# Scores over 64 rows of unpadded keys, a layer norm root per row spread by transposes, two projection units between transposes

## What is computed

```python
hx = rms_norm(x, norm1_g[l]) * (1 + sc1) + sh1
xa_b, xa_c, xa_x, xb_u, xq_g, xk_g, xv_g, xq_w, xk_w, xv_w = split_proj(hx @ w_in[l])
ya, yb = conv_mixers(xa_b, xa_c, xa_x, xb_u, ...)   # yb = silu(layer_norm(dwconv(g) + bias, ln_g, ln_b))
q_g = apply_rope(rms_norm(heads(xq_g), qn_c_g[l]), cos, sin)    # 4 query heads of 64, 2 key heads
o_g = global_attn(q_g, k_g, heads(xv_g), kc_g, vc_g)            # all 512 + 256 keys
o_w = window_attn(q_w, k_w, heads(xv_w), kc_w, vc_w, sink_d[l]) # neighbouring blocks + 256 keys
x = x + g1 * (jnp.concatenate([ya, yb, o_g, o_w], axis=-1) @ w_out[l])
x = x + g2 * hier_moe(rms_norm(x, norm2_g[l]) * (1 + sc2) + sh2, ...)  # 32 experts, 2 per token
```

## Time and profile before

| | us |
|---|---|
| median of 3 runs | 1939.59 (1939.04 to 1943.37) |
| the profiled execution | 1938.68 |
| its span | 1936.8 |
| PE busy | 1672.5 (86%) |
| DVE busy | 689.6 (36%) |
| ACT busy | 322.4 (17%) |
| mean granted TensorE clock | 0.955 of full |

### The profile page before, as it was taken

The page is one execution under the profiler, slowest core; times in us unless marked ns, Lnnn a source line. Parts: engine busy times, 40 slices in busy tenths (PEclk is TensorE's granted clock), DMA queues, the critical chain, the costliest instruction groups (busy, mean ns, idle before and its releaser), DMA issues.

```text
span 1936.8 us, 27043 instructions
## 1 busy us (share of the span) xinstructions
PE 1672.5 (86%) x9982; PEld 985.4 (51%) x9983; DVE 689.6 (36%) x1676; ACT 322.4 (17%) x709; POOL 206.7 (11%) x324
## 2 busy tenths in 40 slices
PE   4999998989969999999795799799969979777773
PEld 2555445754556556665352444476446645444441
DVE  2093655661452212222122477564351111111112
ACT  3110115550210000000000301364110000000000
POOL 0000000000012212222111000000002211111111
PEclk9999998999969999999998799899969999999997
DMA  9347156001259999899998621100169999999994
GB/s 384 143 196 329 66 213 261 1 1 44 92 221 425 426 426 426 341 425 424 428 424 336 246 98 76 44 1 1 76 242 426 425 426 426 425 426 426 426 424 185
DMA packets 51369, 524.57 MB, mean 271 GB/s; under 512 B 10696, under 2 KB 11368, under 8 KB 21872
## 3 DMA queue, kind: packets, MB, share of 16 engines
q1 hardware_dynamic: 33968, 481.51, 59.3%
q0 software_dynamic: 14624, 31.80, 4.3%
q10 hardware_dynamic: 2720, 10.49, 1.4%
HBM read 515.08 MB, written 25.95 MB: 279 GB/s over the span
## 4 chain that ended last, share of the span: by engine, by line
PE 61%; DMA 29%; DVE 7%; ACT 2%; issue 1%; POOL 0%; ACTq 0%; POOLq 0%; DVEq 0%
DMA ring<-in_e_down_dram 25%; PE ps L757 22%; PE ps L534 9%; PE ps L563 7%; PE ps L703 6%; PE ps L598 3%; PE ps L629 2%; PE ps L613 2%; PE ps L484 2%; PE ps L601 2%; DMA xres<-in_ctx_tokens_dram 1%; DMA r<-y_dram 1%; PE ps L745 1%; PE ps L493 1%; PE ps L682 1%
## 5 line engine op out<-in xcount | busy, mean ns | idle before, releaser
L757 PE MATMUL ps<-ring,r 128*64 128x256 f32 (+1 forms) x3920 | 534.2, 427 | 80.4 <-DMA ring<-in_e_up_dram 33.7
L757 PEld LDWEIGHTS ps<-ring,r 128*64 128x64 f32 x3920 | 309.7, 138 | 290.0 <-issue 132.6
L757 PE MATMUL ps<-r 128*64 128x256 f32 (+1 forms) x1760 | 238.2, 423 | 31.7 <-DMA r<-in_e_up_dram 14.1
L1349 DVE TENSOR_TENSOR r<-r,ps 128x128 f32<-128x128 f32 x142 | 34.5, 284 | 540.2 <-PE ps L757 540.2
L757 PEld LDWEIGHTS ps<-r 128*64 128x64 f32 x1760 | 141.1, 137 | 121.0 <-issue 54.5
L534 PE MATMUL ps<-r,ring 128*128 128x512 f32 (+1 forms) x480 | 179.3, 534 | 3.2 <-ACT r L1472 1.6
L563 PE MATMUL ps<-ring,r 128*128 128x512 f32 (+1 forms) x384 | 155.9, 560 | 0.0
L703 PE MATMUL ps<-ring,r 128*128 128x512 f32 x320 | 140.2, 594 | 2.2 <-ACT r L1622 2.2
L534 PEld LDWEIGHTS ps<-r,ring 128*128 128x128 f32 x480 | 92.0, 194 | 93.7 <-issue 87.5
L1369 DVE TENSOR_TENSOR r<-ps,r 128x512 f32<-128x512 f32 x71 | 49.1, 692 | 215.7 <-PE ps L757 215.7
L1645 ACT ACTIVATE r<-ps 128x256 f32<-128x256 f32 x71 | 27.2, 383 | 559.2 <-PE ps L757 559.2
(11 more groups left out here) (192 smaller groups left out, 1480.9 us busy)
## 6 DMA issues: line engine op xcount, KB each, us to landing
ring<-in_e_gate_dram SPq DMA_DIRECT2D x44, 2048.0 KB, 33.1
ring<-in_e_up_dram SPq DMA_DIRECT2D x44, 2048.0 KB, 35.1
ring<-in_e_down_dram SPq DMA_DIRECT2D x44, 2048.0 KB, 35.5
ring<-in_w_mod_dram SPq DMA_DIRECT2D x24, 2048.0 KB, 17.5
r<-in_e_gate_dram SPq DMA_DIRECT2D x20, 2048.0 KB, 35.9
r<-in_e_up_dram SPq DMA_DIRECT2D x20, 2048.0 KB, 38.1
r<-in_e_down_dram SPq DMA_DIRECT2D x20, 2048.0 KB, 38.4
ring<-in_w_in_dram SPq DMA_DIRECT2D x8, 2048.0 KB, 20.4
```

The source lines that it names most:

```text
L757: mm = pe.matmul(ps[g * B:(g + 1) * B, bank, 0:width], x, w[:, k, g * width:(g + 1) * width], start=(k == first), stop=(k == last), tile_p ...
```

## The change

Queries and keys of one head are read from 64 of the 128 partitions of qT and kT with a row tile of the array (`tile_position=(kv * HD, 0)`); `kT_pad`, its clearing and its copies are gone, and the score banks of even and odd units are exchanged. The sums of squares for the layer norm come out as one column per tile with tokens on the rows; root and reciprocal are taken over 128 x 6 elements, and transposes of that column, repeated over 128 columns, spread it behind unit 10 into the banks from which `ln_scale` reads. DVE's two first maxima stand ahead of the rotation of unit 11, and in layer 0 PE's last `mod_turn` stands behind scores 0. In layer 1, units 0 and 1 run on PE between the transposes of tiles 1 and 2 and of tiles 3 and 4, DVE rotates them ahead of `glu_product`, and the ring gets its pieces in the new order. The core of the diff:

```diff
     if layer:
-        return conv + qkv
+        return qkv[:QKV_AHEAD] + conv + qkv[QKV_AHEAD:]
...
+        def score_bank(u):
+            return 2 - u % 2 * 2
...
+                if layer and u < QKV_AHEAD:
+                    pe.wait_ge(h1_act, h1_count(layer, False) + u + 1)
+                    pe.wait_ge(h1_vec, h1_count(layer, True) + u + 1)
...
-                if u >= 1:
+                if u >= (1 + QKV_AHEAD if layer else 1):
                     qk_transposes(layer, u - 1)
...
-                    src = catT[:, 2:4, :]
...
                     pe.wait_ge(ln_sq, 2 * layer + 2)
-                    src = square
+                    for t in range(tiles_of(layer)):
+                        for i in range(2):
+                            mm = pe.matmul(ps[:, 2, t:t + 1], square[:, i, t * P:(t + 1) * P], ones[:, 0:1],
+                                           start=(i == 0), stop=(i == 1))
+                    mm.then_inc(ln_psum, 1)
+                    return
...
                     for i in range(2):
-                        mm = pe.matmul(ps[:, 2 + j, 0:tn], ones, src[:, i, t0:t0 + tn], start=(i == 0), stop=(i == 1))
+                        mm = pe.matmul(ps[:, 2 + j, 0:tn], ones, catT[:, 2 + i, t0:t0 + tn], start=(i == 0), stop=(i == 1))
+                mm.then_inc(ln_psum, 1)
+            def ln_spread(layer):
+                pe.wait_ge(ln_rstds[layer], 1)
+                for t in range(tiles_of(layer)):
+                    mm = pe.transpose(ps_flat[:, 1024 + t * P:1024 + (t + 1) * P],
+                                      ln_rstd[:, t:t + 1].to_broadcast([P, P]), ident)
                 mm.then_inc(ln_psum, 1)
...
-                q = qT[:, group * 2 + r, i * P:(i + 1) * P]
-                bank = (u % 2) * 2
+                rows = slice(kv * HD, (kv + 1) * HD)
+                q = qT[rows, group * 2 + r, i * P:(i + 1) * P]
+                bank = score_bank(u)
...
-                if u == 0 or u == 4:
-                    pe.wait_ge(keys_padded[layer], 2 * (group + 1))
+                if u == 4:
+                    pe.wait_ge(qkT_ready, QKV_UNITS * layer + QKV_UNITS)
...
-                    pe.matmul(ps[:, bank, 512 - w:512], q, kT_pad[:, group, kv, a * P:b * P], start=True, stop=not masks)
+                    pe.matmul(ps[:, bank, 512 - w:512], q, kT[rows, group, a * P:b * P], start=True, stop=not masks,
+                              tile_position=(kv * HD, 0))
                     for m, (at, mask) in enumerate(masks):
                         pe.matmul(ps[:, bank, at:at + P], ident, mask, start=False, stop=m == len(masks) - 1)
-                pe.matmul(ps[:, bank + 1, 0:C], q, kT_pad[:, group, kv, S:TOK], start=True, stop=True).then_inc(s_psum[layer], 1)
+                pe.matmul(ps[:, bank + 1, 0:C], q, kT[rows, group, S:TOK], start=True, stop=True,
+                          tile_position=(kv * HD, 0)).then_inc(s_psum[layer], 1)
...
             def attention(layer):
                 units = units_of(layer)
                 pe.wait_ge(qkT_ready, QKV_UNITS * layer + NT)
-                pe.wait_ge(ln_stds[layer], 1)
+                pe.wait_ge(ln_centred, 3 * layer + 3)
                 scores(layer, 0, units[0])
+                if layer == 0:
+                    mod_turn(12 * DEPTH - 1)
+                    pe.wait_ge(mod_ready, 4)
                 scores(layer, 1, units[1])
                 qk_transposes(layer, QKV_UNITS - 1)
-                pe.wait_ge(qkT_ready, QKV_UNITS * layer + QKV_UNITS)
...
-                        if layer:
-                            h1_transposes(layer, 0, NT)
                         started = True
                     if kind == "conv":
+                        if layer and n == CONV_ORDER[0]:
+                            h1_transposes(layer, 2 * QKV_AHEAD, NT)
                         conv_projection(layer, n)
+                        if layer and CONV_AT[n] < QKV_AHEAD:
+                            qk_transposes(layer, CONV_AT[n])
                     if kind == "qkv":
+                        if layer and n < QKV_AHEAD:
+                            h1_transposes(layer, 2 * n, 2 * n + 2)
                         qkv_projection(layer, n)
                         if n in (LN_MEAN, LN_VAR):
                             ln_sums(layer, 0 if n == LN_MEAN else 1)
-                    if turned is not None:
+                        if n == LN_VAR + 1:
+                            ln_spread(layer)
+                    if turned is not None and turned < 12 * DEPTH - 1:
                         mod_turn(turned)
                         turned = None
...
-                if layer == 0:
-                    pe.wait_ge(mod_ready, 4)
                 last_pT = attention(layer)
...
+            def ln_root(layer):
+                t = tiles_of(layer)
+                ve.wait_ge(ln_stds[layer], 1)
+                nc.vector.reciprocal(ln_rstd[:, 0:t], ln_rstd[:, 0:t]).then_inc(ln_rstds[layer], 1)
             def ln_scale(layer):
-                n = S + (C if layer == 0 else 0)
-                ve.wait_ge(ln_stds[layer], 1)
-                own(nc.vector.reciprocal(ln_std[:, 0:n], ln_std[:, 0:n]))
-                settle()
+                n = tiles_of(layer) * P
+                ve.wait_ge(ln_psum, 3 * layer + 3)
                 for i in range(2):
-                    nc.vector.tensor_tensor(catT[:, 2 + i, 0:n], catT[:, 2 + i, 0:n], ln_std[:, 0:n],
+                    nc.vector.tensor_tensor(catT[:, 2 + i, 0:n], catT[:, 2 + i, 0:n], ps_flat[:, 1024:1024 + n],
                                             ALU.mult).then_inc(ln_centred, 1)
...
                 tokens_in(layer)
                 clear_pads(layer)
+                if layer:
+                    for u in range(QKV_AHEAD):
+                        rotate(layer, u)
                 glu_product(layer)
                 for tap in range(TAPS_EARLY):
                     conv_b_tap(layer, tap)
@@ -1408,16 +1440,22 @@
...
                 for u in range(QKV_UNITS):
-                    if layer == 0 and u == QKV_UNITS - 1:
-                        mod_copy(1, MOD_CONV - 12, 12, turned_bank(MOD_CONV), 24)
-                    rotate(layer, u)
+                    if u == QKV_UNITS - 1:
+                        unit_max(layer, 0, units_of(layer)[0])
+                        if layer == 0:
+                            mod_copy(1, MOD_CONV - 12, 12, turned_bank(MOD_CONV), 24)
+                        unit_max(layer, 1, units_of(layer)[1])
+                    if layer == 0 or u >= QKV_AHEAD:
+                        rotate(layer, u)
                     if TAPS_EARLY + u < TAPS_B:
                         conv_b_tap(layer, TAPS_EARLY + u)
+                    if u == LN_VAR + 1:
+                        ln_scale(layer)
                     store_qk(layer, u)
                     if u == LN_MEAN:
                         ln_centre(layer)
                     if u == LN_VAR:
-                        ln_scale(layer)
+                        ln_root(layer)
                 amplitude(layer, "norm2", 4 * KD, 2)
...
-                if u == 0:
+                if u == (QKV_AHEAD if layer else 0):
                     ac.wait_ge(conv_mul, 2 * layer + 2)
...
             def ln_roots(layer):
-                n = S + (C if layer == 0 else 0)
-                ac.wait_ge(ln_psum, 2 * layer + 2)
-                nc.scalar.activation(ln_std[:, 0:n], ps_flat[:, 1024:1024 + n], ACT.Sqrt, bias=eps,
+                t = tiles_of(layer)
+                ac.wait_ge(ln_psum, 3 * layer + 2)
+                nc.scalar.activation(ln_rstd[:, 0:t], ps[:, 2, 0:t], ACT.Sqrt, bias=eps,
                                      scale=1.0 / W_CF).then_inc(ln_stds[layer], 1)
...
-            def pad_keys(layer, group):
-                ac.wait_ge(qkT_ready, QKV_UNITS * layer + NT * (group + 1))
-                ac.wait_ge(qkv_psum, QKV_UNITS * layer + QKV_UNITS)
-                ac.wait_ge(keys_zeroed[layer], 4)
-                for half, kv in ((slice(0, HD), 0), (slice(HD, P), 1)):
-                    nc.scalar.copy(kT_pad[half, group, kv, :], kT[half, group, :]).then_inc(keys_padded[layer], 1)
             def attention(layer):
                 units = units_of(layer)
-                pad_keys(layer, 0)
+                ac.wait_ge(qkv_psum, QKV_UNITS * layer + QKV_UNITS)
                 unit_exp(layer, 0, units[0])
                 unit_exp(layer, 1, units[1])
-                pad_keys(layer, 1)
                 for u in range(0, len(units), 2):
...
-                po.wait_ge(qkv_psum, QKV_UNITS * layer + QKV_UNITS)
-                for group in range(2):
-                    nc.gpsimd.memset(kT_pad[HD:P, group, 0, :], 0.0).then_inc(keys_zeroed[layer], 1)
-                    nc.gpsimd.memset(kT_pad[0:HD, group, 1, :], 0.0).then_inc(keys_zeroed[layer], 1)
```

More of the change, by code:

```diff
@@ L62 @@
 QKV_UNITS = 2 * NT
+QKV_AHEAD = 2
 CONV_ORDER = (6, 7, 8, 9, 0, 1, 2, 3, 4, 5)
@@ L182, in hybrid_flow_block @@
         rstd = sb("rstd", [P, NT])
```

(12 more changed lines are left out.)

## The result

The change makes the kernel slower: 1955.8 us median (1951.98 to 1957.8) against 1940.0 (1939.04 to 1943.37), ratio 1.0076 with the 95% interval 1.0062 to 1.0089. The profiled execution took 1957.56 us with a span of 1955.7, that of before 1938.7 with 1936.8. The forecast was 1940.4 and the range ended at 1951: the time lies outside, on the slow side.

What follows compares the result with a forecast made beforehand. PE was taken to bound most of the chain (61%), with waits at layer 1's entry and the turns to attention. Gains of -23.2 and +24.9 for attention's mode changes net +1.7: 1940.4 us, whole range 1914 to 1951.

Steps and rivals of the forecast that it cites:

- The first term: Layer 0, turn from projections to attention: new norm form and scores without padding start `attend` 0 earlier, -4.2 us.
- The second term: Layer 1, the same turn from projections to attention: `attend` starts at 1244.4 instead of 1252.60, -8.2 us.
- The third term: Layer 1 entry: projection units 0 and 1 between the transposes fill time in which PE waits, -10.8 us.
- the price of attention: Both layers' attention: changes between 64-row score tiles and full-array products cost PE time, +24.9 us together.
- the edges in the latent tiles: Latent-tile attention: mode changes cost 3.0 us a tile, 24.0 over eight tiles, less 0.9 for the first two units.
- the context tiles: Layer 0 attention: mode changes cost 1.8 us in each context tile, half counted because PE idles there, +1.8 us.
- in the new hole: Start of attention: the first two units run where PE would otherwise wait, so 0.9 us of mode-change cost drops out.
- an excursion from full array to tiles and back costs 0.30 us: Attention scores: 0.30 us per round trip, read from column tiles and assumed for row tiles; half beside `weigh`.
- The rival built on it: Attention scores: row tiles cost more, 0.44 us an excursion, 36.5 us in all, time 1952.0 us; chance 0.15.
- the dearer edge: Attention scores: the case of 0.22 us for one edge, net +13.3 us, time 1952.0 us; chance 0.15.

Runs made afterwards that it cites:

- x2: The kernel after, but scores over all 128 rows again, with POOL copying each unit's queries into half-zero slots: 1920.0 us, ratio 0.9901.
- x4: x2 with the two projection units moved back behind the entry of layer 1, none between its transposes: 1933.5 us, ratio 0.9958.
- y4: x2 with 64-row tiles for the scores of the window group only: 1940.9 us, ratio 1.0006.
- y1: x2 with the layer norm's old form (sums over ones, root and reciprocal on all tokens, no spreading transposes): 1926.0 us, ratio 0.9920.
- x3: The kernel after with the window group's masks behind both score products instead of between them: 1948.2 us, ratio 1.0037.
- y3: The kernel after with the first four units of each layer's attention scored over all 128 rows from padded queries: 1943.7 us, ratio 1.0018.
- x1: The kernel before with only its score products on 64-row tiles, the padded keys still made and waited for: 1978.1 us, ratio 1.0190.

## Why the prediction was wrong, point by point

**The first term was right.** -4.2 forecast. `attend` 0 came only 1.8 earlier; but the run was 0.6 us late at 250 us already, where nothing of this term has begun, and lost 1.7 to a fall of the clock at 285 (last section). 313.2 + 0.6 + 1.7 = 315.5 against 315.61: the term is -4.1. Three kernels without that fall confirm it: from the first sums of the norm to `attend` 0 stand 155.8 us in x2, x4 and y4, against 160.05 before. The working was right in the exponential as the last link, and about right in what the norm's new form costs there (1.8 us forecast, 1.2 by y1).

**The second term was right**: -8.2 forecast, -8.1 measured. From the sums of the mean to `attend` 0 stood 41.8 us before (1210.78 to 1252.60) and stand 33.7 after (1219.35 to 1253.04). y1 gives the reciprocal 3.7 of it.

**The third term was right within 1 us**: -10.8 forecast, -9.9 measured. A fall of the clock lies in it, behind PE's wait of 2.11 us (window of the kernel after, all engines):
```profile
1200.20:1203.60 3.40, 3.40 (x10) 2.69 (x9) 2.90 (x9) 0.30 (x1) 0.00 (x0) 0.50 0.00 0
```
It cost little: the stretch takes 134.9 to 135.3 us in the four kernels with units ahead that have it (after, x3, y1, y4) and 134.8 to 134.9 in x2 and y3, which have not. The conv units start 2.4 us later relative to the first transposes (1088.76 and 1109.63, the transposes at 1065.60 and 1084.11), 3.7 had been forecast; PE waits 2.11 us behind unit 4, forecast 2.0. x4 confirms the term from the other side.

The three together: -22.1 measured, -23.2 forecast.

**The failed step is the price of attention, +24.9 forecast and +35.2 measured, and it failed in two terms.** Between the starts of the same `weigh`, pair of units by pair, the 35.2 come apart so: 25.6 for the edges in the latent tiles (12.8 in either layer; forecast 24.0 less 0.9), 8.6 for the clock (forecast nothing) and 1.0 for the context tiles (forecast 1.8).

**The larger term was put at nothing: the clock that stays down.** The prediction let the first two units run "in the new hole" and took 0.9 off. In fact PE stayed at 1.2 GHz through its first 10.8 and 12.0 us of attention, where before it had come back after 3.1 in either layer. The first two pairs lost 5.4 us in layer 0 and 5.9 in layer 1 (10.84 before, 16.75 after); less 1.6 for their edges, that is 3.7 and 4.3 for the clock. Another 0.6 went in layer 0's last `weigh`, where the clock fell again at 442.5. y3 shows that most of it goes with full-array products at the start. The prediction asked whether PE's clock would fall in a hole; it did not ask whether it comes back behind it.

**The other is "an excursion from full array to tiles and back costs 0.30 us".** That an excursion costs at all was right. The Trainium skill ("TensorEngine Tiling (Array Packing)", Key Properties) says that changing the mode drains TensorE. For row tiles x1, x2 and x3 now show a price: 0.15 to 0.19 us at most changes of mode. The size was taken from `weigh`, whose products load only 64 columns and have transposes as neighbours. Both make an edge cheap: 0.09 + 0.05 going in, 0.10 + 0.06 coming out. `scores` and masks are fp32 products with 128-column loads, and pay 0.09 + 0.10 at nearly every edge. By the rows above an unmasked even unit loses 0.35 (0.30 forecast), an odd one 0.20 (0.15), a masked even one 0.74 (0.60), a masked odd one 0.59 (0.45). These sum to 3.76 a tile; it lost 3.56 instead of 3.0. In one global pair PE had waited 0.1 us before, so that the global group lost 0.94, near the 0.90 forecast; the window group, with its masks, lost 2.62 instead of 2.10.

Four times 3.56 in a layer would be 14.2, and 12.8 were measured, since 3.56 is the loss of a tile in the middle. Scores 0 and 1 stand ahead of `attend` 0 (0.5 less), the two global pairs of the second tile lose only 0.3 each (0.3 less), two window pairs 1.23 instead of 1.31, and the last pair of the last tile, in which PE had waited 1.1 us for ACT before, is now 0.45 us shorter.

The right row stood in the prediction: 0.22 for the edge at L534, which has such a load. The rival built on it gave 1952.0 and was given 0.15. That its 36.5 us come near the 35.2 is luck: edges and context tiles make 26.6 of these, and the clock, which it did not hold either, the rest. What the 0.10 goes with is what stands behind the edge: it is there behind 32-column tiles (L534) as behind 64-row ones, and the loads of those products take 0.19 us, where those of transposes and of `weigh` take 0.13 to 0.14.

**The context tiles** were forecast at +1.8, half of 3.6 hidden. Their eight pairs took 23.6 us before and 24.7 after: 1.0, so more than two thirds of the 3.6 are hidden by the loop through ACT.

In the sum: attention +25.6 edges, +8.6 clock, +1.0 context = 35.2, forecast 24.9. The difference between the forecast (1940.4) and the profiled execution (1957.56) is 17.2 us: 10.3 here, 1.1 short in the three gains, 1.7 + 0.4 + 1.4 at places that the sum left at nothing, and the 0.6 + 1.7 ahead of the turn in layer 0. The range was too narrow for the same reasons: its upper end, 1951, stopped short even of the dearer edge's 1952.0, and nothing in it stood for a clock that stays down.

**What stays open.** What in the 64-row products keeps the clock down is not settled. The kernel after, x3 and x1 all show it, though x1 has nothing else of the change; x2, y3 and y4 do not; y4 starts with the global group over all rows. In the six cases (three kernels, two layers) the clock came back 2.1 to 5.3 us behind the start of the first `weigh`; whether it is `weigh` that brings it back was not tried, nor was a longer run of 64-row products with no mode edges among them. The falls of the clock at 442.5 (kernel after) and 1316.3 (x2) are not explained either.

## What to carry to other kernels

Count the changes of tiling mode in the order in which TensorE meets them, masks and transposes included, and price each by what stands behind it: here 0.19 us ahead of an fp32 product with a 128-column load, nearly what a record of 256 columns takes, and 0.15 ahead of transposes. A smaller contraction that saves no columns buys nothing, so pad the small operand on an idle engine (POOL, 0.28 us a unit) and leave the array in one mode. And after each pause of TensorE look at the clock not only in the pause but in the first products behind it.

## What the runs showed of the hardware

- **The price of a mode change.** 0.09 us between the last record of one mode and the first of the next, and 0.10 more ahead of the second record of an fp32 product with a 128-column load, 0.06 where transposes follow, 0.05 where products with 64-column loads follow. Rows and columns alike, both ways. Between products of one mode there is none (the 512- and the 256-column product of an unmasked unit).
- **A clock that stays down under full load.** 0.50 for 13.6 us (kernel after, either layer) and 0.51 over 11.7 us of unbroken work (x1), where with full-array products in the same place it was 1.00 within 2.5 to 5.0 us of `attend` 0 (before, x2, y3). It cost 8.0 us here.
- **A fall of the clock behind products with one moving column.** Timeline of PE, the kernel after:
```profile
280.61 2.74 PE L584 MATMUL ps<-const,r 128*128 128x1 f32 x24
284.17 2.44 PE L488 MATMUL ps<-ring,cond 128*32 128x512 f32 x16
```
and its windows:
```profile
283.40:286.60 3.20, 3.20 (x25) 1.24 (x24) 2.18 (x6) 0.26 (x1) 0.00 (x0) 0.82 0.00 0
286.60:290.00 3.40, 3.40 (x7) 1.57 (x7) 0.00 (x0) 0.59 (x1) 0.00 (x0) 0.67 0.00 0
```
PE does not pause, yet the clock falls; 0.18 x 3.2 + 0.33 x 3.4 is 1.7 us lost. It was seen in the kernel after, in x3 and in y3, and not in x2, x4 and y4, which have the same 24 products. With the old form of the norm (before, x1, y1) it was not seen in this place. It seems to be a matter of chance, and no run here settles it.
